# Gate and up projections by seven Strassen products, and a down projection that is summed in one go

## The reference

```python
h = h + 0.5 * rmsnorm(swiglu(rmsnorm(h, g0), w_gate, w_up, w_down), g1)
u = rmsnorm(h, g2)                 # one projection of u, then pool, attention and conv branches
h = h + rmsnorm(merge_of_gated_branches(u) @ w_out, g3)
h = h + 0.5 * rmsnorm(swiglu(rmsnorm(h, g4), ...), g5)
# swiglu(x) = (silu(x @ w_gate) * (x @ w_up)) @ w_down
```

## Time and profile before

| | |
|---|---|
| Time, median of 3 runs | 2793.59 us (2792.86 to 2795.0) |
| Profiled execution, span (the page gives no other time of it) | 2795.9 us |
| PE busy | 2757.9 us (99%), 18682 matmuls |
| DVE, ACT, POOL busy | 1245.5, 849.1, 447.1 us (45%, 30%, 16%) |
| DMA | 208.44 MB, mean 75 GB/s |

### The profile page before, as it was taken

How to read it: one execution, slowest core, us unless ns; L and a number is a source line. 1 busy time by engine, 2 the same in 40 slices (tenths; PEclk the granted TensorE clock), 3 DMA queues, 4 the chain that set the end, 5 groups by cost and what they waited for, 6 DMA issues and landing times.

```text
span 2795.9 us, 54256 instructions
## 1 busy us (share of the span) xinstructions
PE 2757.9 (99%) x18682; PEld 2719.4 (97%) x18682; DVE 1245.5 (45%) x1997; ACT 849.1 (30%) x1331; POOL 447.1 (16%) x473
## 2 busy tenths in 40 slices
PE   8999999999999999999999999999999999999998
PEld 8999999989999999999999999999899999999997
DVE  5332333674444733233453333355644455333335
ACT  4221223333333522122332122233333343212223
POOL 3100112240001410011321001132300032100112
PEclk9999999999999999999999999999999999999998
DMA  3232222122223222222222222221122222222222
GB/s 104 75 90 86 73 82 71 48 61 66 74 73 91 59 73 81 66 75 87 65 70 75 83 83 75 86 73 50 46 75 75 77 76 61 75 83 76 74 79 89
DMA packets 425146, 208.44 MB, mean 75 GB/s; under 512 B 42425, under 2 KB 423323, under 8 KB 424987
## 3 DMA queue, kind: packets, MB, share of 16 engines
q1 hardware_dynamic: 421956, 203.46, 25.3%
q10 hardware_dynamic: 3062, 3.38, 0.4%
HBM read 203.28 MB, written 5.29 MB: 75 GB/s over the span
## 4 chain that ended last, share of the span: by engine, by line
PE 94%; DVE 3%; issue 1%; ACT 0%; POOL 0%; DVEq 0%; DMA 0%; SPq 0%; ACTq 0%; POOLq 0%
PE ps L540 30%; PE ps L541 29%; PE ps L542 29%; DVE h L1198 1%; DVE x_lo L1180 1%; PE ps L593 1%; PE ps L641 1%; PE ps L588 1%; PE ps L589 1%; PE ps L663 1%; PE ps L521 1%; DVE w_lo L1162 0%; PE ps L527 0%; POOL acc_y L1580 0%; PE ps L691 0%
## 5 line engine op out<-in xcount | busy, mean ns | idle before, releaser
L540 PE MATMUL ps<-x_hi,w_hi 128*128 128x320 f32 x3648 | 1136.6, 312 | 0.0
L542 PE MATMUL ps<-x_hi,w_lo 128*128 128x320 f32 x3648 | 1127.2, 309 | 0.0
L541 PE MATMUL ps<-x_lo,w_hi 128*128 128x320 f32 x3648 | 1127.0, 309 | 0.0
L540 PEld LDWEIGHTS ps<-x_hi,w_hi 128*128 128x128 f32 x3648 | 684.8, 188 | 11.4 <-issue 6.5
L541 PEld LDWEIGHTS ps<-x_lo,w_hi 128*128 128x128 f32 x3648 | 685.0, 188 | 0.2
L542 PEld LDWEIGHTS ps<-x_hi,w_lo 128*128 128x128 f32 x3648 | 684.8, 188 | 0.0
L858 ACT ACTIVATE w_hi<-raw 128x1024 fp32r<-128x1024 f32 (+1 forms) x326 | 362.3, 1114 | 758.8 <-PE ps L542 758.8
L1162 DVE TENSOR_TENSOR w_lo<-raw,w_hi 128x1024 fp32r<-128x1024 f32 (+1 forms) x326 | 423.4, 1300 | 179.9 <-ACT w_hi L858 179.9
L540 PE MATMUL ps<-mid_hi,w_hi 128*128 128x320 f32 x1232 | 382.0, 310 | 0.0
L541 PE MATMUL ps<-mid_lo,w_hi 128*128 128x320 f32 x1232 | 380.7, 309 | 0.0
L542 PE MATMUL ps<-mid_hi,w_lo 128*128 128x320 f32 x1232 | 380.7, 309 | 0.0
(11 more groups left out here) (199 smaller groups left out, 3001.1 us busy)
## 6 DMA issues: line engine op xcount, KB each, us to landing
raw<-in_ffn_w_gate_dram SPq DMA_DIRECT2D x360, 128.0 KB, 2.2
raw<-in_ffn_w_up_dram SPq DMA_DIRECT2D x360, 128.0 KB, 2.3
raw<-in_w_in_dram SPq DMA_DIRECT2D x304, 128.0 KB, 2.2
raw<-in_ffn_w_down_dram SPq DMA_DIRECT2D x192, 192.0 KB, 2.7
raw<-in_ffn_w_down_dram SPq DMA_DIRECT2D x64, 128.0 KB, 2.8
raw<-in_w_branch_dram SPq DMA_DIRECT2D x64, 128.0 KB, 2.6
raw<-in_w_out_dram SPq DMA_DIRECT2D x64, 128.0 KB, 2.3
rows<-in_x_prompt_dram SPq DMA_DIRECT2D x4, 512.0 KB, 5.3
```

Of the source, the lines that this page charges most:

```text
L540: pe.matmul(bank(b), wh, tile(xh, k, hf), start=k == ks[0], stop=False)
L541: pe.matmul(bank(b), wh, tile(xl, k, hf), start=False, stop=False)
L542: mm = pe.matmul(bank(b), wl, tile(xh, k, hf), start=False, stop=k == ks[-1])
```

## The change

**Gate and up.** Two column tiles of gate, or two of up, are one unit; the first two tiles of each still come from `first_four`, so 20 units (`UNITS`) are left in a block. With k split in two halves of 4 tiles (`QK`), tokens in halves 0 and 1 and columns in two tiles, a unit is a 2 x 2 by 2 x 2 block product. It is made by Winograd's form of Strassen's method, of seven products (P1 to P7) with 4 x 3 = 12 matmuls each.

- The left side needs eight more hi/lo tiles for the sums S1, S2 (and four for S4, four for the difference S3). They are made once in a block: `sums12` and `sum4` on VectorE, `sum_hi` and `s3_high` on ScalarE, `difference` and `sum_low` on GpSimd, `s3_low` on VectorE.
- Each unit needs four sums of weights T1 to T4 of 512 columns (`t_first`, `t_second` on VectorE, `t_high` on ScalarE, `t_low` on GpSimd), beside the split of the weights that are used as they are (`w0_high`, `w0_low` of 1024 columns, `b22_high` and one more `t_low` of 512).
- Three intermediate sums are copied out of PSUM by ScalarE (`snap` 1, 2, 3); the next product adds to the same bank and waits for the copy. VectorE adds the four results up from PSUM and a copy, multiplies them by `inv_x`, and after silu multiplies gate by up.

**Down.** All 22 `mid` tiles are kept in float32. When gate and up are done they are split (22 hi/lo pairs a half), and down sums over all 22 in PSUM: 66 matmuls a group, weights in chunks of 8, 7 and 7 k tiles in a ring of four slots. Nothing is added in SBUF.

**Around it.** Raw buffers and weight slots are four; `states` is issued in the mixer, between the second half's `x` tiles and its roots; `wp_now` is loaded there by DMA; the wait for `kv_stored` moves from ScalarE behind the merge loop to VectorE ahead of it. The products of the mixer, and `sums`, `spread` and the places of both in `first_four`, stay.

The core of the diff:

```diff
+UNITS = NF - 2
+QK = KD // 2
+PRODS = 7 * UNITS
 # PE
+            def product(what, u, lhs, b, begin):
+                slot, k0 = {"P1": (0, 0), "P2": (0, QK), "P6": (1, 0), "P5": (1, QK), "P7": (2, 0), "P4": (2, QK),
+                            "P3": (3, QK * (u % 2))}[what]
+                for k in range(QK):
+                    ...                      # three matmuls: wh x hi, wh x lo, wl x hi
+                mm.then_inc(prod, 1)
+                def body(u, at):
+                    pe.wait_ge(snap1, b20 + at + 1)
+                    if first:
+                        pe.wait_ge(s_lo, ss0 + 2 * QK)
+                    product("P6", u, lambda part, k: s_op(1, part, k), a, False)
+                    ...
+                    product("P5", u, lambda part, k: s_op(0, part, k), d, True)
+                    pe.wait_ge(snap2, b20 + at + 1)
+                    ...
+                    product("P7", u, s3, a, False)
+                    if not last:
+                        p1(u + 1, at + 1)
+                    pe.wait_ge(snap3, b20 + at + 1)
+                    product("P4", u, a22, a, False)
+                    if not last:
+                        p2(u + 1, at + 1)
+                    pe.wait_ge(c22_out, b20 + at + 2)
+                    product("P3", u, lambda part, k: s_op(2, part, k), d, False)
 # ScalarE, one unit, then the head of a block
+                    if gate:
+                        silu(gate_scaled, gs0 + i * 3 + 1, i * 2 + 2, 0)
+                    snap(2, u, at)
+                    if not last:
+                        b22_high(u + 1, 1 + nxt, old("P3", 1) if u else None)
+                    if not gate:
+                        silu(gate_scaled, gs0 + i * 3 + 3, i * 2 + 3, 0)
+                    snap(3, u, at)
+                    if not last:
+                        t_high(u + 1, "T2", at + 1, old("P6"))
+                        t_high(u + 1, "T1", at + 1, old("P5"))
+                        t_high(u + 1, "T3", at + 1, old("P7"))
+                        snap(1, u + 1, at + 1)
+                        t_high(u + 1, "T4", at + 1, old("P4"))
+                    if gate:
+                        silu(gate_scaled, gs0 + i * 3 + 2, i * 2 + 3, 1)
+                        silu(c21_out, b20 + at + 3, i * 2 + 2, 1)
+                ...                          # w0_next: w0_high of unit u + 2, after P2 of unit u + 1
+                x_second(sm - 1, l, 4 * n)
+                for k in range(QK):
+                    act.activation(part_s[k][:, :], tile(h, QK + k, 1), ACT.Copy, ...).then_inc(a22_made, 1)
+                head_silu(0, 0)
+                for i in range(4):
+                    sum_hi(i)
+                head_silu(1, 0)
+                for i in range(4, 8):
+                    sum_hi(i)
+                x_norm_second(sm - 1)        # roots(BX[1], n, 3), keep_inv_x(1, n)
+                w0_high(0, 1, (group_done, g + 5))
+                head_silu(0, 1)
 # VectorE, one unit, then the head of a block
+                def body(u, at, i):
+                    w0_low(u + 1, at + 1)
+                    first_quarters(u, at, i)     # c12 of u-1 and c11 of u: add, add, scale, scale, times up
+                    t_first(u + 1, at + 1, 1 + (i + 1 if u % 2 else i))
+                    t_second(u + 1, at + 1)
+                    last_quarters(u, at, i)      # c22: add, scale; c21: scale
+                x_second(sm - 1, l, 4 * n)
+                scale(tile(mid, 0, 0), 0, 0, g)
+                scale(up[0][:, :], 1, 0, g + 1)
+                sums12(0)                        # two scalar_tensor_tensor, the second reads the first
+                scale(tile(mid, 1, 0), 2, 0, g + 2)
+                sums12(1)
+                head_mid(0, 0)
+                scale(up[1][:, :], 3, 0, g + 3)
+                sums12(2)
+                head_mid(1, 0)
+                sums12(3)
+                second_half(sm - 1)              # inverse(n, 3), wait for inv_x_made
+                t_first(0, 0, 1)
 # GpSimd
+                x_squares(sm - 1)
+                for k in range(QK):
+                    difference(k)
+                for i in range(2 * QK):
+                    sum_low(i)
+                for j, what in enumerate(("T2", "T1", "T3", "T4")):
+                    t_low(what, 0, j + 1)
+                ...
+                with pool.Fori(0, UNITS // 2 - 1) as i:
+                    unit_low(1, i * 2 + 1)       # B22, T2, T1, T3, T4: 512 columns each
+                    unit_low(2, i * 2 + 2)
+                for k in range(0, NF, 2):        # the lo parts of the even mid tiles, half 1
+                    ...
 # the end of gate and up on ScalarE; VectorE has chunk_low, mid_low and the last quarters in like order
+                chunk_high(0, (prod, p0 + prod_no("P2", u)))
+                for k in range(5):
+                    mid_high(k, 0)
+                snap(2, u, u)
+                ...
+                snap(3, u, u)
+                ...
 # mixer on ScalarE
-                begin(sm - 1, l, 2)
+                x_second(sm - 1, l, 2)
+                states(l)
+                x_norm_second(sm - 1)
```

More of the change, by code:

```diff
@@ L193, in trunk_kernel @@
+        assert 32 * P <= 4 * HB
+        tb = [own(f"tb{s}", HT) for s in range(3)]
+        inv_x = [own(f"inv_x{s}", HT) for s in range(2)]
         ident, ones = own("ident", P), own("ones", P)
@@ L596, in first_four @@
                     for s in range(2):
-                        group(pair + 1, g + 4 * hf + 2 + s, s, 2 + s, (x_hi, x_lo), K8, hf,
-                              lambda k: stand((hf, "all", 2 + s, k)), "first")
-            def last_four(pair, g, n, x, ks, where):
-                long = len(ks) == FG
-                for q in range(8):
-                    c = q % 4
-                    def between(k):
-                        if (q, k) == (4, 5):
-                            sums(acc_y[0], BY[0], SQUARES * (n + 1) + 2 + 12)
-                        if (q, k) == ((4, 9) if long else (5, 1)):
-                            spread(BY[0], 4 * (n + 1))
-                    group(pair + c // 2, g + q, c % 2, c, x, ks, q // 4, between, "main" if c < 2 else where)
@@ new lines, in silu, with old @@
+                def silu(sem_, v, f, hf):
+                    act.wait_ge(sem_, v)
+                    alone(act)
+                    act.activation(at_tile(mid, f, hf), at_tile(mid, f, hf), ACT.Silu).then_inc(silu_done, 1)
+                def body(u, at, i):
+                    def old(what, back=0):
+                        return prod, p0 + (prod_no(what, at - back) if isinstance(at, int) else prod_at(what, at - back))
+                    gate = u % 2 == 0
+                    last = u == UNITS - 1
+                    nxt = i + 1 if u % 2 else i
+                    if gate:
[15 more added lines that the diff above has]
+                        silu(c21_out, b20 + at + 3, i * 2 + 2, 1)
@@ L1214, in seam, with put_y, x_second, second_half @@
-            def seam(n, y, add, pair, g, nk, where, pl, pn, gl, gn):
-                def take(q):
-                    put_y(tile(y, KD // 2 + q % 4, q // 4), q % 4, g, q, add)
+            def put_y(dst, b, done):
+                dve.wait_ge(*done)
+                dve.tensor_copy(dst, bank(b)).then_inc(evac, 1)
+            def x_second(n, gl, gn):
+                for j in range(8, 16):
+                    x_low(j, n + 1, gl, gn)
+                dve.wait_ge(inv_x_made, 2 * (n + 1) + 1)
+            def second_half(n):
+                inverse(n, 3)
+                dve.wait_ge(inv_x_made, 2 * (n + 1) + 2)
@@ L1556, in _ @@
             dve.wait_ge(ident_in, 16)
-            stage(1, 0, KD, "first")
-            stage(1, 1, KD, "first")
+            for s in range(2, 4):
+                stage(s + 1, s, KD, s)
             inverse(-1, 2)
```

1398 lines of the change are left out of this document (906 added, 492 removed).

## The result

The kernel with the change is slower, by 0.3%. Its median is 2803.78 us (2802.16 to 2805.56, 6 runs), that of the kernel before, on the same chip, 2794.22 us (2792.86 to 2798.46, 6 runs). The ratio is 1.0032, with a 95% interval from 1.0021 to 1.0042. The profiled execution has a span of 2803.5 us for 2795.9, which is 7.6 us more.

What follows compares the result with a forecast made beforehand. It took PE to bound the kernel: 2795.9 - 140.8 (matmuls) + 8 (loop) + 47.8 (head) + 20 (clock) + 19 (down) + 1 (rest) = 2750.9 us profiled, 2749 us as median, range 2688 to 2796.

Steps and rivals of the forecast that it cites:

- points 1: Gate and up matmuls: 240 fewer in each block, 960 in all at 0.1467 us, -140.8 us.
- Point 3: Head of a block: PE stands waiting because the second half's inverse comes behind the new sums, +47.8 us.
- 5: From the last unit into down: PE waits for snap 3 and split mid lo parts, +19 us, between 0 and 40.
- the loop's pitch: Sign: same loop instruction returns after 24.6 to 25.3 us for two units; prediction fails if off by over 0.5 us.
- Point 2: Gate and up loop: PE stays the bound, a gate unit loses about 0.2 us, an up unit nothing; +8 us.
- Point 6: The rest: states ahead of the roots costs +1 us; loads, kv_stored wait and the seam's other stalls nothing.
- Point 4: Clock behind the head stalls: 5.1 us lost after each of four stalls, +20 us, between 0 and 24.
- The shared-port one: Rival: port shared by VectorE and GpSimd bounds the loop, 1.6 us a gate unit, 2844 us in all; 11%.

Runs made afterwards that it cites:

- Run 1: Kernel with the change, with the second half's inverse and root moved ahead of the sums in the four heads; 2787.21 us, ratio 0.9973.
- run 6: Kernel with the change, inverse first, s3_high ahead of sum_hi 6 and 7, second-half scales, s3_low and w0_low(1) ahead of sum4; 2787.91 us, ratio 0.9973.
- 9: Kernel with the change, inverse first, all sums12 ahead of w0_low(0), snap 1 behind T1, s3_high behind T3, B22 ahead of third sums; 2781.34 us, ratio 0.9962.
- 12: Kernel with the change, with the head order of 9, snap 2 ahead of silu in gate units, an earlier last take, unit 0's snap 2 early; 2732.17 us.
- Run 8: Kernel with the change, with VectorE's last take of down ahead of the third weight tile's lo part and two x_lo; 2791.37 us, ratio 0.9988.
- run 5: Kernel with the change, plus 40 unused matmuls ahead of the second half's spread in the four gate and up heads; 2801.93 us, ratio 1.0028.
- run 4: Kernel with the change, GpSimd making gate and up lo parts for 128 of 512 columns only (output not the reference's); 2762.29 us, ratio 0.9885.
- large filler: Kernel with the change, plus 76 unused matmuls ahead of the second half's spread in heads behind the mixer, 60 in the others; 2817.07 us, ratio 1.0075.

## Why the prediction was wrong

It forecast 2749 (2688 to 2796); the time was 2803.78. The mechanisms of points 1, 3 and 5 were there. Against the profiled execution the sum failed by 52.6 us. The loop, the first units and the seams hold 55.2 of it (20.5, 24.1 and 10.6 over what was forecast), the head 3.5 and down 3.0, and the clock gives 9.1 back. One of its own signs came true: the loop's pitch, forecast as 24.84 us for two units with 0.5 as the limit, was 25.45.

- **Point 2, the loop: +8 forecast, +28.5 measured.** The tight place was named rightly (w0_high, w0_low behind T4, adds, scales, silu, snap 2), and its price was too low. I put the end of GpSimd's T4 at 12.1 of the unit, with five parts of 1.2 us each and `w0_low` at 1.23. In the kernel after, T1, T3 and T4 each began beside a VectorE instruction and took 1.54. T4 ended at 12.7, and `w0_low`, which had to wait for its turn, at 1.5 of the next unit and not at 0.9. So 0.81 a gate unit and not 0.2. I had used hindered durations in the head, and not in the loop. My sums for each engine (8.4, 6.5 and 6.0 us under 12.32) said that no engine was full, which was true and did not matter.
- **Point 2 again, the first units: nothing forecast, +24.1.** I ran the chain in its steady state alone. In unit 0 snap 1 stands behind s3_high, and snap 2 behind a silu that waits for `s3_low` and `w0_low(1)`. By starts PE loses 1.7 to 2.0 us at P6(0) and 2.4 at P7(0) in each block, and the rest to the clock behind that. Runs 1, 6, 9 and 12 show that this place takes over when the head is mended.
- **Point 6, the seams: "the same on paper" (+1 for `states`), +11.6.** They were not the same in the program. In the kernel before, the last take stands behind three `x_lo`. In the kernel after it stands behind a weight tile (1.21 us) and two `x_lo` more. It begins at 496.41, 2.9 us behind the last matmul that PE has ahead of the sums; before it began 0.4 behind:

```profile
496.41 0.47 DVE L1584 COPY u<-ps 128x320 f32<-128x320 f32 x1
...
498.26 0.48 DVE L1206 TENSOR_TENSOR y_ffn<-ps,y_ffn 128x320 f32<-128x320 f32 x1
```

  Run 8, which only moves it, takes 8.0 of these 11.6 us back by starts.
- **Point 4, the clock: +20 forecast, +10.9 measured.** I took 5.1 us a head from the windows behind the stall at 497.8; behind these stalls a head lost 3.0. Where run 5 gave some of it back, a wait for ScalarE came behind it. This is an error to the good side.
- **Points 3 and 5 were near:** 51.3 for 47.8, and 22.0 for 19. In point 3 five more `x_lo` at 0.60 are 3.0 us and not the 2.3 that were added, which is 1.4 of the difference.

Point 3 was right in its size, the order of the inverse and the count of hindered instructions. But what it meant was not: I took the stall for the price of one misplaced step. Run 1 took that step away and got a third of it back, because the sums, parts and copies behind it fill the engines until P7(0).

Of the rivals none came about as told. The shared-port one had the right cause and the wrong size; it needed 1.3 us a gate unit to be slower, and the change became slower at 0.8, through places that no rival had. What failed in it was not the lock. The exclusive lock of the Trainium skill ("SBUF — State Buffer", Who interferes with whom) fits this trace, in which the later instruction ends a fixed time behind the other one's end (0.35, 0.55 and 1.08 us, for 0.49, 0.69 and 1.23 alone). The rival had 1.6 us because it let T4 end at 13.4 and `w0_low` at 2.3, where they ended at 12.7 and 1.5. And the 8.53 us of the earlier trace rows, which I held against the lock, can't speak against it: only three of the eight `x_lo` stand beside squares there. Those three come 1.09 us apart, by turns: an `x_lo` ends 0.35 behind a square, the square 0.74 behind the `x_lo`.

## What to carry over

Run the chain through the first and the last turn of a loop too, not only the steady one. Where VectorE and GpSimd both read two SBUF operands, let them take turns in the timeline on paper, and do not use means: 1.59 us was a mixture of 1.23 and 1.95, and the one that stood in the chain was the long one. Check the releaser that a profile names against the semaphore values that the instruction waits for; in run 6 it named the wrong engine and sent the next experiment to the wrong step. A stall at the head of a stage is worth its length only if the work behind the late step is on time; list what each engine still owes to the first products before counting it as a gain. Copies that free or feed PE belong ahead of whatever waits for another engine, which here brought 36 us for one moved line.

## What was not expected of the hardware

- VectorE and GpSimd take turns by whole instructions when both read two SBUF operands. Only the one that begins later is lengthened, and it saves a constant part: the VectorE instruction ends 0.13 to 0.15 us earlier than its full length behind the other's end, whether it has 320, 512 or 1024 columns (0.35 for 0.49, 0.55 for 0.69, 1.08 for 1.23), and GpSimd's of 512 columns ends 1.16 behind VectorE's for 1.30. With GpSimd's instructions of 128 columns in run 4 it is the same: 0.32 for 0.46.
- In the kernel with the large filler the granted clock was 0.50 from 954 to 958, after three idle gaps of 0.6 us at the `x_lo` waits (from 950.4 to 953.1), although fillers kept PE busy from 954.56 on; it was 1.00 again at 960.
